# A hybrid decoder step on one core: the first program reordered, and the first norm's scale and shift moved out of it into the attention

## The chip, the cores and the metric

One core of a Trainium2 chip runs the whole kernel. The time is device microseconds of one execution. A core has five engines that run their own instruction lists and meet at semaphores: TensorE (PE; PEld is its weight load), VectorE (DVE), ScalarE (ACT), GpSimd (POOL) and SyncE (SP), which here only issues transfers. All engines read and write the on-chip memory SBUF; TensorE writes its results into eight PSUM banks.

## The reference, cut to what matters

One decoder layer for 1,040 prompt rows (16 learned ones ahead of 1,024) and 64 sample rows, all of width 1024, in float32. What the change touches is the first layer norm, the input projection and the three mixers that read it:

```python
xp = layer_norm(concat([meta, x_prompt]), ln0_g, ln0_b)   # (x - mu) * rsqrt(var + eps) * g + b
z = x @ w_in                       # q, k, v (512 each), 8 forget logits, u (256), p (256)
logf = log_sigmoid(z_f + b_f)
att = softmax(q k^T * scale + cum(logf)_i - cum(logf)_j, causal) @ v
ys  = state-space mixer of u       # y = gelu(scan(u)); y * sigmoid(y @ w_glu + b_glu)
yq  = window means of p (2, 4, 8, 16) minus p, times w_pool
h = layer_norm(alpha * x + concat([att, ys, yq]) @ w_out, ...)
out = layer_norm(alpha * h + moe(h), ...)   # 16 experts, 2 a row
```

Note that the normed rows `x` are used twice: at once by the projection, and much later in the residual `alpha * x`.

## The kernel before, in words

The rows are cut into nine tiles of 128 (`NT = 9`, the last one only 80 rows full). Three programs follow each other, each with its own instruction list for every engine, written out by hand; a program starts when all engines have ended the one before.

**The first program.** For each tile: SP loads the rows into one of six slots `xin`; VectorE takes mean and variance (`stats`), ScalarE the square root, VectorE the reciprocal and the bias (`centre` on DVE), ScalarE writes (x - mu) * rstd in place (`centre` on ACT). TensorE transposes the eight 128-column blocks (`turn_x`), and ScalarE copies the transposed blocks into `xT` and applies gain and shift there, where they are one number per partition (`copy_out`). So the projection reads `xT`. For the residual, GpSimd multiplies the rows in `xin` by the gain and adds the shift, both as 128x1024 operations with vectors spread over all partitions (`gb`), and SP then stores the tile to the DRAM buffer `x_park` and reuses the slot for a later tile.

Between the tiles TensorE runs the projections of u and p (`project(c, u)`, three chunks of 384 columns by four units, the last chunk with 48 columns of padding) and the forget logits (`forget_parts`, `forget_sum`). Then come the value projections (`values(t)`, nine of them), four groups of transposes of the state-space input matrix `Wbd` into `WT` (semaphore `s_wt`, emptied by ScalarE under `s_wc`), 128 small products for the matrix `Tm` (`s_tb`), and sixteen sums of the inputs into states (`s_in`, emptied by ScalarE under `s_ic`), which need GpSimd's rearranged copy `U4` of u (`s_u4`). VectorE makes the matrices (`block_matrices`), a table of rotations (`turns`, ended by `s_tn`), the forget logits (semaphore `s_z`) and their running sums (`s_lf`, `s_cum`), and, when all sixteen sums are in, turns them, scans over time and turns back (ended by `s_xs`). TensorE then makes the eight outputs (`s_y`), ScalarE their GELU (`s_ge`); the pooling mixer's product and the gate follow.

**The second program** is the attention: four pairs of heads, and in each nine row tiles. GpSimd makes, for every tile and head, the diagonal block `diag` (gate sums plus causal mask), four of them deep; VectorE adds scores and gate sums (line 1630, the last piece reads `diag`), ScalarE takes exponentials. Into tiles 2 to 7 of a pair TensorE puts the six projections of the next pair's keys and queries (line 1419), whose weights GpSimd loads at tile 0 (lines 1323, 1324). TensorE's score banks form a ring of four, emptied by VectorE.

**The third program** has the output projection, the residual with the rows of `x_park`, the second norm, the experts and the last norm.

## Time and profile before

| | us |
|---|---|
| median of 3 runs (lowest, highest) | 1066.41 (1066.04, 1068.19) |
| the profiled execution, its own time | 1070.63 |
| its span, first to last instruction | 1068.9 |
| first program ends | 258.1 |
| attention ends | 552 |
| TensorE busy / VectorE / ScalarE / GpSimd | 925.8 / 459.0 / 325.9 / 216.9 |

The profile shows one execution. Times in the rows are from the start of the span. A row of the timeline gives the start, the length, the engine, the line, what is written and read, the shapes and how many instructions it joins; in square brackets stands how long the engine sat idle before it, and what ended that.
### The profile page before, as it was taken

The numbers are of one execution on the slowest core, as the hardware profiler recorded it, in microseconds if no ns is written. First come the engines' busy times: TensorE is split into PE (matmuls) and PEld (weight loads), VectorE is DVE, ScalarE is ACT, GpSimd is POOL, SyncE is SP. The second block draws the span as 40 slices with busy tenths as digits, with TensorE's granted clock in tenths as the row PEclk, the third lists the DMA queues.
The fourth block names the chain that finished last, engine by engine and source line by source line (L and its number), as shares of the span: only waits on it lengthen the run. The fifth ranks groups of instructions, "written<-read, shape, count | busy, mean of one in ns | idle before, by whom it ended". The sixth has DMA issues, their size and how long they took to land. (4 is left out here: it accounts for less than half of the span.)

```text
span 1068.9 us, 13692 instructions
## 1 busy us (share of the span) xinstructions
PE 925.8 (87%) x5012; PEld 587.2 (55%) x5012; DVE 459.0 (43%) x1270; ACT 325.9 (30%) x657; POOL 216.9 (20%) x285
## 2 busy tenths in 40 slices
PE   2689949797989999999889999996799999999491
PEld 2454535364546665666564444442588787878140
DVE  3679956961234434434652243746300100001076
ACT  6462032173123323333532333333112121211322
POOL 4748910000110200200120001232100000000274
PEclk9889969999989999999999999999799999999796
DMA  9513001013992300300731211257776888965382
GB/s 241 152 57 119 1 3 40 29 52 116 423 426 60 96 15 1 101 1 1 241 138 59 80 41 40 97 189 306 257 250 222 308 321 281 373 218 216 127 330 110
DMA packets 63214, 164.05 MB, mean 153 GB/s; under 512 B 19209, under 2 KB 28464, under 8 KB 57640
## 3 DMA queue, kind: packets, MB, share of 16 engines
q1 hardware_dynamic: 57287, 141.90, 38.2%
q0 software_dynamic: 5856, 21.24, 5.5%
q8 instruction: 42, 0.69, 0.3%
q14 instruction: 29, 0.23, 0.1%
HBM read 108.65 MB, written 54.52 MB: 153 GB/s over the span
## 5 line engine op out<-in xcount | busy, mean ns | idle before, releaser
L1419 PE MATMUL banks<-xT,arena 128*128 128x384 f32 (+1 forms) x384 | 126.5, 486 | 10.6 <-DVE mx L1630 4.1
L2086 PE MATMUL banks<-arena,mixT 128*128 128x512 f32 x288 | 131.6, 603 | 0.0
L1419 PEld LDWEIGHTS banks<-xT,arena 128*128 128x128 f32 x384 | 72.8, 193 | 62.3 <-issue 11.5
L2086 PEld LDWEIGHTS banks<-arena,mixT 128*128 128x128 f32 x288 | 52.9, 192 | 56.2 <-issue 56.2
L1538 ACT ACTIVATE arena<-arena,mx 128x128 f32<-128x128 f32 (+8 forms) x72 | 58.5, 813 | 65.6 <-DVE mx L1630 65.0
L2250 PEld LDWEIGHTS banks<-mixT,v_tok 128*128 128x128 f32 x512 | 72.4, 194 | 4.5 <-issue 4.5
L2250 PEld LDWEIGHTS banks<-mixT,arena 128*128 128x128 f32 x512 | 70.4, 190 | 6.8 <-issue 6.8
L2250 PE MATMUL banks<-mixT,v_tok 128*128 128x160 f32 x512 | 73.0, 304 | 0.8 <-ACT mixT L2454 0.8
L2250 PE MATMUL banks<-mixT,arena 128*128 128x160 f32 x512 | 71.7, 300 | 0.8 <-ACT mixT L2454 0.8
L2596 POOL DMA_INDIRECT arena<-y_park,slot_i x18 | 17.2, 956 | 257.7 <-DMA y_park<-arena 252.6
L499 PE MATMUL banks<-xT,v_tok 128*128 128x384 f32 x192 | 66.3, 502 | 2.6 <-ACT xT L691 2.6
L1317 POOL TENSOR_TENSOR diag<-arena,causal 128x128 f32<-128x128 f32 (+1 forms) x72 | 30.3, 430 | 186.9 <-DVE mx L1630 180.4
L2859 DVE TENSOR_TENSOR mixT<-arena,banks 128x320 f32<-128x320 f32 x16 | 7.8, 488 | 131.8 <-PE banks L2250 131.8
L529 PE MATMUL banks<-mixT,xT 128*128 128x512 f32 x144 | 62.6, 593 | 0.0
L2263 PE MATMUL banks<-arena,mixT 128*128 128x512 f32 x128 | 57.6, 593 | 0.9 <-DVE arena L2847 0.9
L1450 PE MATMUL banks<-ident,arena 128*128 128x128 f32 (+1 forms) x360 | 47.6, 265 | 7.9 <-ACT arena L1538 2.9
L499 PEld LDWEIGHTS banks<-xT,v_tok 128*128 128x128 f32 x192 | 36.8, 196 | 30.2 <-issue 5.2
L2847 DVE COPY arena<-banks 128x512 f32<-128x512 f32 x20 | 13.8, 691 | 91.1 <-PE banks L2263 65.5
L1450 PEld LDWEIGHTS banks<-ident,arena 128*128 128x128 f32 (+1 forms) x360 | 36.4, 139 | 24.9 <-issue 9.9
L1439 PE MATMUL banks<-arena 64*128 64x512 f32 (+5 forms) x240 | 48.3, 504 | 1.6 <-DVE mx L1630 1.6
L2562 POOL TENSOR_TENSOR xT<-xT,gb 128x1024 f32<-128x1024 f32 x9 | 21.2, 2354 | 133.7 <-DVE xT L2639 133.7
L1630 DVE CUSTOM_DVE_ANT_0 arena<-banks,arena 128x512 f32<-128x512 f32 (+4 forms) x64 | 36.1, 587 | 27.7 <-PE banks L1439 27.4
(393 smaller groups left out, 1403.3 us busy)
## 6 DMA issues: line engine op xcount, KB each, us to landing
arena<-in_w_down SPq DMA_DIRECT2D x16, 1024.0 KB, 8.1
x_slots<-xT SPq DMA_DIRECT2D x4, 2048.0 KB, 22.4
y_park<-xT SPq DMA_DIRECT2D x4, 2048.0 KB, 42.8
v_tok<-in_w_gate SPq DMA_DIRECT2D x8, 1024.0 KB, 6.0
v_tok<-in_w_up SPq DMA_DIRECT2D x8, 1024.0 KB, 6.2
arena<-in_w_gate SPq DMA_DIRECT2D x8, 1024.0 KB, 5.8
arena<-in_w_up SPq DMA_DIRECT2D x8, 1024.0 KB, 6.9
arena<-x_slots SPq DMA_DIRECT2D x16, 512.0 KB, 5.0
```

What stands on the lines that cost most here:

```text
L499: last = T.matmul(bank[2 + n % 2][:, 0:cn], w[:, k, m * P:(m + 1) * P], xT[:, k, c0:c0 + cn], start=(k == 0), stop=(k == KD - 1))
L529: last = T.matmul(bank[t % 2][:, :], xT[:, k, t * P:(t + 1) * P], w_v[:, k, :], start=(k == 0), stop=(k == KD - 1))
L1317: G.tensor_tensor(diag[:, n % 4, 0:w], nb[i % 2][:, h, t * P:t * P + w], causal[:, 0:w], ALU.add).then_inc(s_dg, 1)
L1419: last = T.matmul(b[:, 0:cn], w[:, k, :], xT[:, k, c0:c0 + cn], start=(k == 0), stop=(k == KD - 1))
L1439: T.matmul(b[0:nq(t), 0:w], qT[i % 2][r, t * P:t * P + nq(t)], kT[i % 2][r, c0:c0 + w], start=True, stop=True).then_inc(s_ring, 1)
L1450: last = T.transpose(b[0:w, j * q:(j + 1) * q], sc[(NT * i + t) % 2][h][0:q, kb * P:kb * P + w], ident[0:q, 0:q])
L1538: S.activation(row, row, ACT.Exp, bias=mx[0:q, 2 * t + h, len(parts(t)) - 1:len(parts(t))], scale=-1.0, accum_out=lsum[0:q, 2 * t + h:2 * ...
L1630: ins = V.tensor_tensor_reduce(sc[(NT * i + t) % 2][h][0:q, k0:k0 + kn], b[0:q, k0 - c0:k0 - c0 + kn], row, -1.0, 3.0e38 if first else mx[ ...
L2086: last = T.matmul(bank[half], mixT[:, k, t * P:(t + 1) * P], w_oh[half][:, k, :], start=(k == 0), stop=(k == KD - 1))
L2250: last = T.matmul(bank[2 * (e % 2) + which][:, CAP * j:CAP * (j + 1)], w_gu[e % 2][:, DW * which + k * DE + j * P:DW * which + k * DE + (j ...
L2263: last = T.matmul(bank[6 + half], hid[e % 6][:, j, 0:MAIN], w_dn[e % 5][:, j * D + 512 * half:j * D + 512 * half + 512], start=(j == 0), s ...
L2562: G.tensor_tensor(h_all[:, t, :], h_all[:, t, :], gb[:, 1, :], ALU.add).then_inc(s_h, 1)
```

## The change

Five things are changed.

1. The first program no longer applies gain and shift to the rows in `xin`: its eighteen GpSimd operations and the two loads of the spread vectors go. SP stores a tile to `x_park` when it is centred, without them.
2. In the attention, GpSimd loads each parked tile back into a piece of the arena, multiplies, adds, and stores it again: one tile behind the diagonals of each of nine row tiles, from tile 2 of the first pair to tile 1 of the second. Two slots are used in turn. The piece is the place of half of the output weights `w_oh[0]`, whose load moves from the start of the attention to the third pair.
3. On VectorE the tile statistics are taken ahead of the state-space parameters (`angles`, `powers`, `input_gain`, `input_matrix`), and the copies of `pick_rows` go to ScalarE. The forget logits move from behind the table of rotations into it, and the running gate sums behind the scan. The reciprocals of `fix` move behind that.
4. On TensorE the transposes of `Wbd` and the products for `Tm` stand ahead of the first two value projections, and three later value projections move one place back: the one after the `Tm` products behind the sixteen sums, `values(7)` behind the fourth output and `values(8)` behind the sixth. ScalarE's copies follow.
5. The last projection chunk has 336 columns and not 384 (the padding is left out).

The core of the diff:

```diff
@@ SP, first program @@
-                sp.dma_start(gb[:, 0, :], bcast_rows(A["ln0_g"], P)).then_inc(s_gain, 16)
-                sp.dma_start(gb[:, 1, :], bcast_rows(A["ln0_b"], P)).then_inc(s_shift, 16)
...
                 for t in range(NT):
-                    sp.wait_ge(s_normed, t + 1)
+                    sp.wait_ge(s_cen, t + 1)
                     sp.dma_start(x_park[t], xin[t % XSL]).then_inc(s_stored[t % XSL], 16)
@@ GpSimd, first program @@
-                for t in range(NT):
-                    pool.wait_ge(s_turned, 2 * t + 2)
-                    G.tensor_tensor(xin[t % XSL], xin[t % XSL], gb[:, 0, :], ALU.mult).then_inc(s_gained, 1)
-                    pool.wait_ge(s_gained, t + 1)
-                    G.tensor_tensor(xin[t % XSL], xin[t % XSL], gb[:, 1, :], ALU.add).then_inc(s_normed, 1)
-
-                pool.wait_ge(s_normed, NT)
+                pool.wait_ge(s_turned, 2 * 6)
@@ TensorE: project, and behind the projections @@
-                    c0, cn = CHUNKS[c]
+                    c0, cn = CHUNKS_T[c]
...
-                pe.wait_ge(s_wv, 16)
-                values(0)
-                values(1)
                 pe.wait_ge(s_bm, 2)
-                pe.wait_ge(s_free, len(ORDER))
                 for b in range(4):
+                    pe.wait_ge(s_free, len(ORDER) - 1 + b if b < 2 else len(ORDER))
...
                     last.then_inc(s_wt, 1)
...
+                    if b == 1:
+                        pe.wait_ge(s_fpc, 3)
+                        blocks_T(0)
+                blocks_T(1).then_inc(s_tb, 1)
+                pe.wait_ge(s_wv, 16)
+                values(0)
+                values(1)
                 pe.wait_ge(s_u4, 1)
...
-                for t in range(3, 8):
+                for t in range(2, 7):
                     values(t)
...
                     if q == 3:
+                        values(7)
+                    if q == 5:
                         values(8)
@@ ScalarE, behind the projections @@
+                for b in range(4):
+                    act.wait_ge(s_wt, b + 1)
+                    S.copy(WT[:, 2 * b:2 * b + 2, :, :].rearrange("p q r n -> p (q r n)"),
+                           bank[2 + b % 2][:, :]).then_inc(s_wc, 1)
                 act.wait_ge(s_z, 1)
...
                 values(0)
                 values(1)
-                for b in range(4):
-                    act.wait_ge(s_wt, b + 1)
...
@@ VectorE: in turns(), and the new functions @@
                     while n < CHP:
+                        if n == P:
+                            logits()
...
+                def logits():
...
+                    dve.wait_ge(s_fs, 3)
+                    for c in range(3):
+                        last = V.tensor_scalar(lf[:, 384 * c:384 * (c + 1)], bank[6][32 * c:32 * c + H, 0:384],
+                                               bfc[:, 0:1], None, ALU.add)
+                    last.then_inc(s_z, 1)
@@ GpSimd, attention @@
+                def load_parked(m):
+                    if m >= 2:
+                        pool.wait_ge(s_po[m % 2], 16 * (m // 2))
+                    pool.dma_start(park[:, 2 + m % 2, :], x_park[m]).then_inc(s_pi[m % 2], 16)
+
+                def normed(m):
+                    if 1 <= m < NT - 1:
+                        load_parked(m + 1)
...
+                    pool.wait_ge(s_pi[m % 2], 16 * (m // 2 + 1))
+                    x = park[:, 2 + m % 2, :]
+                    G.tensor_tensor(x, x, park[:, 0, :], ALU.mult).then_inc(s_pg, 1)
+                    pool.wait_ge(s_pg, m + 1)
+                    G.tensor_tensor(x, x, park[:, 1, :], ALU.add).then_inc(s_ps, 1)
+                    pool.wait_ge(s_ps, m + 1)
+                    pool.dma_start(x_park[m], x).then_inc(s_po[m % 2], 16)
+
+                load_parked(0)
+                load_parked(1)
...
                             n += 1
+                        if 2 <= NT * i + t < NT + 2:
+                            normed(NT * i + t - 2)
                         if t == 0 and i < 3:
                             pool.wait_ge(s_ring, of_rows[i, 5] + 1)
```

How the instructions stand on the engines, at three places. First TensorE, from the last projections (written to banks 2 and 3) to the state sums (to banks 2, 3, 6, 7). Before:

```order
L499 MATMUL banks_3<-xT,v_tok 128x384 x24
L529 MATMUL banks_1<-mixT,xT 128x512 x16
L591 MATMUL banks_3<-ident,arena 128x128 x16
L598 MATMUL banks_5<-arena 32x128 x2
...
L529 MATMUL banks_1<-mixT,xT 128x512 x8
L612 MATMUL banks_3<-arena 128x276 x2
```

and now:

```order
L485 MATMUL banks_3<-xT,v_tok 128x336 x16
L584 MATMUL banks_3<-ident,arena 128x128 x8
L523 MATMUL banks_5<-arena 32x128 x2
...
L584 MATMUL banks_3<-ident,arena 128x128 x8
...
L515 MATMUL banks_1<-mixT,xT 128x512 x16
L602 MATMUL banks_3<-arena 128x276 x2
```

The value projections (128x512) that stood on both sides of the transposes (128x128) and of the `Tm` products (32 rows) now stand behind both, and there are two ahead of the sums and not three.

Second VectorE in the first norm, around tiles 3 to 5 (statistics into `ln_st`, parameters in `par`). Before:

```order
L824 TENSOR_SCALAR ln_st<-ln_st 128x1
L987 COPY pick<-ident 8x8 x4
L828 TENSOR_TENSOR par<-par 128x8
L846 TENSOR_SCALAR par<-par 128x8
...
L855 TENSOR_SCALAR par<-par 128x16
L815 BN_STATS ln_st<-arena 128x6
```

and now:

```order
L822 TENSOR_SCALAR ln_st<-ln_st 128x1
L813 BN_STATS ln_st<-arena 128x6
...
L826 TENSOR_TENSOR par<-par 128x8
L844 TENSOR_SCALAR par<-par 128x8
...
L853 TENSOR_SCALAR par<-par 128x16
L821 RECIPROCAL ln_st<-ln_st 128x1
```

The four copies and the ten operations on the angles stood between tile 3 and the statistics of tile 4; the copies are gone from this engine, and the angles stand behind the statistics of tile 5.

Third GpSimd in the attention's first pair (`diag` are the diagonals, `arena<-in_w_in` the weights of the next pair). Before:

```order
L1317 TENSOR_TENSOR diag<-arena,causal 128x128 x2
L1323 DMA arena<-in_w_in 128x8x128
L1324 DMA arena<-in_w_in 128x8x128
L1317 TENSOR_TENSOR diag<-arena,causal 128x128 x14
```

and now:

```order
L1341 TENSOR_TENSOR diag<-arena,causal 128x128 x4
L1325 TENSOR_TENSOR arena<-arena 128x1024
L1327 TENSOR_TENSOR arena<-arena 128x1024
L1329 DMA x_park<-arena 128x1024
L1341 TENSOR_TENSOR diag<-arena,causal 128x128 x2
L1315 DMA arena<-x_park 128x1024
L1325 TENSOR_TENSOR arena<-arena 128x1024
```

Where fourteen diagonals followed each other, each tile's two are now followed by a load, two operations of 1,024 columns and a store.

## Rows read from the trace of the kernel before

**Rows 1.** Busy time by stretch: length; busy PE, PEld, DVE, ACT, POOL; clock; DMA

```profile
25.90:119.30 93.40, 79.89 (x296) 45.62 (x297) 76.06 (x193) 37.44 (x81) 67.80 (x83) 0.93 0.31 96
...
134.10:149.40 15.30, 0.06 (x1) 0.00 (x0) 8.35 (x26) 7.66 (x9) 4.06 (x9) 0.60 0.00 0
...
171.30:212.80 41.50, 35.20 (x91) 15.57 (x90) 40.74 (x48) 4.21 (x6) 0.00 (x0) 0.95 0.13 45
...
242.00:258.10 16.10, 12.07 (x32) 6.59 (x32) 3.16 (x6) 7.87 (x14) 0.00 (x0) 0.89 0.03 8
```

**Rows 2.** Timeline of TensorE (start, length, what), one projection and one tile's transposes

```profile
75.19 1.04 PE L484 MATMUL banks<-ident,mixT 128*128 128x128 f32 x8
...
90.92 5.43 PE L499 MATMUL banks<-xT,v_tok 128*128 128x384 f32 x16
```

**Rows 3.** Groups of TensorE, first program, by form: the forget-gate products

```profile
L511 PE MATMUL banks<-xT,w_f 128*32 128x384 f32 x48 | 4.9, 532 | 0.0
...
L522 PE MATMUL banks<-arena,pick 128*8 128x384 f32 x6 | 2.4, 488 | 0.3 <-ACT arena L715 0.3
```

**Rows 4.** Timeline of the first norm, around its tile 4

```profile
36.21 2.35 POOL L455 TENSOR_TENSOR mixT<-mixT,gb 128x1024 f32<-128x1024 f32 x1
...
36.38 2.20 DVE L849 TENSOR_SCALAR par<-par 128x8 f32<-128x8 f32 x1
...
43.51 0.20 ACT L681 ACTIVATE ln_st<-ln_st 128x1 f32<-128x1 f32 x1 [8.77 <-DVE ln_st L818]
```

**Rows 5.** Timeline of TensorE between the projections and the state sums

```profile
119.38 13.90 PE L529 MATMUL banks<-mixT,xT 128*128 128x512 f32 x32
...
149.41 1.97 PE L591 MATMUL banks<-ident,arena 128*128 128x128 f32 x8 [15.25 <-ACT arena L768]
...
151.31 5.04 PE L598 MATMUL banks<-arena 128*32 128x128 f32 x128
...
163.25 7.60 PE L612 MATMUL banks<-arena 128*128 128x276 f32 x32
```

**Rows 6.** Timeline of VectorE and ScalarE around the forget logits

```profile
139.76 1.85 DVE L1024 TENSOR_SCALAR gb<-banks,bfc 8x384 f32<-8x384 f32 x3 [0.26 <-DVE en L840]
...
141.65 1.16 ACT L761 ACTIVATE ncum<-gb 8x1152 f32<-8x1152 f32 x1 [21.56 <-DVE gb L1024]
...
156.49 4.00 DVE L1041 COPY arena<-banks 32x512 f32<-32x512 f32 x8 [4.03 <-PE banks L598]
...
160.52 2.19 DVE L1047 SCALAR_TENSOR_TENSOR arena<-ident,dcol,arena 128x128 f32<-128x128 f32 x8
```

**Rows 7.** Groups of GpSimd, first program: the copies into U4

```profile
L468 POOL COPY arena<-arena 32x96 f32<-32x96 f32 (+1 forms) x96 | 46.5, 485 | 4.0
```

**Rows 8.** Timeline of ScalarE, the last four GELUs

```profile
229.67 0.59 ACT L719 COPY v_tok<-banks 128x512 f32<-128x512 f32 x1 [2.38 <-PE banks L529]
...
231.36 10.64 ACT L781 ACTIVATE arena<-banks 32x276 f32<-32x276 f32 x16 [1.11 <-PE banks L633]
```

**Rows 9.** Timeline of the attention, its first two pairs

```profile
290.48 2.50 POOL L1317 TENSOR_TENSOR diag<-arena,causal 128x128 f32<-128x128 f32 x6
...
298.70 8.18 PE L1419 MATMUL banks<-xT,arena 128*128 128x384 f32 x16 [3.39 <-DMA arena<-in_w_in]
...
357.69 0.89 POOL L1323 DMA_DIRECT2D arena<-in_w_in  x1 [13.88 <-PE banks L1419]
...
370.88 0.35 DVE L1630 CUSTOM_DVE_ANT_0 arena<-banks,diag,mx 128x128 f32<-128x128 f32 x1
...
372.85 5.43 PE L1419 MATMUL banks<-xT,arena 128*128 128x384 f32 x16
```

**Rows 10.** DMA issues: operation, number, size, median us from issue to landing

```profile
x_park<-mixT SPq DMA_DIRECT2D x7, 512.0 KB, 2.9
...
arena<-in_w_in POOLq DMA_DIRECT2D x2, 512.0 KB, 12.5
...
x_slots<-xT,slot_i POOLq DMA_INDIRECT x18, 4.8
```

More of the change, by code:

```diff
@@ L531, in values, with blocks_T @@
                     last.then_inc(s_vm, 1)
+                def blocks_T(h):
+                    for q in range(4 * h, 4 * h + 4):
+                        for j in range(L):
+                            for r in range(2):
+                                last = T.matmul(
+                                    bank[4 + h][32 * j:32 * j + 32, (q % 4) * P + 32 * j:(q % 4 + 1) * P],
+                                    Wbd[:, r, q, 32 * (L - 1):32 * L], CA[:, r, q, 0:32 * (L - j)],
+                                    start=(r == 0), stop=(r == 1))
+                    return last
                 pe.wait_ge(s_ids, 1)
@@ L635, in _ @@
                     if q == 3:
+                        values(7)
+                    if q == 5:
                         values(8)
+                pe.wait_ge(s_lf, 1)
+                for t in range(NT):
+                    last = T.transpose(bank[2][:, t * H:(t + 1) * H], lf[:, t * P:(t + 1) * P], ident[0:H, 0:H])
+                last.then_inc(s_lft, 1)
                 pe.wait_ge(s_vc, NT)
@@ L719, in values @@
                     S.copy(v_tok[:, t, :], bank[t % 2][:, :]).then_inc(s_vc, 1)
+                act.wait_ge(s_ids, 1)
+                act.wait_ge(s_wz, 3)
+                for g in range(4):
+                    last = S.copy(pick8[32 * g:32 * g + H, :], ident[32 * g:32 * g + H, 32 * g:32 * g + H])
+                last.then_inc(s_pk, 1)
                 centre(0)
@@ L1000, in _ @@
                 centre(3)
-                pick_rows()
-                angles()
                 stats(4)
@@ L1131, in _ @@
                 dve.wait_ge(s_free, len(ORDER))
+                dve.wait_ge(s_g, 1)
+                chain(V.reciprocal(fix[:, :, :], fix[:, :, :]))
+                for g, w in enumerate((2, 4, 8, 16)):
+                    f = fix[64 * (g % 2):64 * (g % 2) + 64, g // 2, :]
+                    last = V.tensor_scalar(f, f, float(w), None, ALU.mult)
+                chain(last)
                 shifted(la, line[:, 0, :], 1)
```

97 lines of the change are left out of this document (38 added, 59 removed).

## The prediction

> **What bounds the kernel now.** The chain that ended last reaches back only into the third program, so the first program and the attention are read by stretches first: how long a stretch is, and which engine fills it [rows 1]. From the first projection to the last one (25.90 to 119.30) no engine is full: TensorE 79.9 of 93.4 us, VectorE 76.1, GpSimd 67.8. There the timeline shows who waits for whom. GpSimd's gain or shift of one tile lasts 2.35 us, and a VectorE operation on 128x8 numbers that starts in it lasts 2.20 us and ends with it; ScalarE then stands 8.77 us for VectorE's statistics [rows 4]. So VectorE is held up by GpSimd, ScalarE by VectorE, and TensorE, which needs ScalarE's centred rows and copies, by all three.
>
> The second stretch is idle TensorE: 15.3 us between the two first value projections and the transposes of `Wbd`, released by ScalarE's copies out of the banks [rows 1, 5]. The timeline of the other engines says why those are late: ScalarE sits 21.56 us in front of the exponential of the forget logits, for which VectorE's logits end at 141.6; the copies stand behind that in ScalarE's list [rows 6]. In the third (171.30 to 212.80) VectorE is the bound, 40.7 of 41.5 us, while TensorE makes value projections. The fourth ends the program in 16.1 us [rows 1]. In the attention's first pairs TensorE bounds; GpSimd has 2.50 us of diagonals for three tiles and is otherwise idle [rows 9].
>
> **The change, stage by stage.** I compare where each stage ends, since work that only moves inside one costs nothing.
>
> *A, the projections (end 119.3).* With GpSimd's eighteen operations gone, and the angles behind the statistics, I take it that rows, statistics and copies keep ahead of TensorE from the second chunk on, so that the stage lasts as long as TensorE's work. Eight projections at 5.43 us are 43.4; four with 336 columns are 4 x 5.43 x 336/384 = 19.0; six tiles' transposes at 1.04 us are 6.2 [rows 2]; the forget products are 4.9 and 2.4 [rows 3]. Sum 75.9, and 2.5 us for copies that TensorE must still wait for at the tile where ScalarE does its two extra rounds (an estimate, somewhat over one 2.35 us step of the old chain [rows 4]). End 25.9 + 78.4 = 104.3, which is 15.0 earlier. The bounds: TensorE busy 79.9 less 2.7 of padding against 93.4 gives at most 16.2; if the waits on ScalarE and VectorE stay, only the padding and the 2.35 us that VectorE stands in front of an angle operation go, about 5.
>
> *B, to the end of the sixteen sums (170.9).* Before: 119.3 to 170.9, 51.6 us. After, TensorE does sixteen transposes at 1.04 per eight (the 1.97 in the row stands behind the idle time, in a stretch where the granted clock was 0.60 [rows 1, 5]), 2.1; the `Tm` products 5.04; two value projections 13.9; the sums 7.6. Together 28.6, end 132.9. That is 38.0 earlier, of which 15.0 come from A and 23.0 are new: the idle 15.25, a value projection of 13.90/2 = 6.95 that now stands behind, and about 0.9 of transposes. The covers: `U4` costs GpSimd 46.5 us [rows 7]; even if it begins only when eight of the twelve projections are done, two thirds through A near 78, it ends at 125, and the sums want it at 132.9 - 7.6 = 125. VectorE's logits begin at 139.8 [rows 6]; 15.0 earlier, and earlier by the waits for GpSimd too (2 at least, one like that in [rows 4]), makes 122; behind them stand 1.85 of logits and the 4.00 + 2.19 of `Tm` (together 8.0) [rows 6], end 130 to 132. This cover is thin (1 to 3 us): what VectorE lacks there is paid one for one.
>
> *C, VectorE's scan.* 41.5 us before and after [rows 1]: its end moves from 212.8 to 174.8. TensorE has five value projections beside it as before, which fill 35.2 of the 41.5.
>
> *D, outputs and GELU.* Before, the last GELU ended at 242.0, 29.2 after the scan [rows 8]. After, two value projections stand among the outputs. Behind the first of them the fifth GELU starts as before 231.4 - 212.8 = 18.6 after the scan, when its output is there; the sixth output follows in about 1.8 (an estimate: some four products like the sums', which took 7.60/16 each [rows 5]), then value projection 8 with 6.95, the seventh output with 1.8, and two GELUs of 10.64/4 = 2.66: 34.5. So D loses 5.2, rounded. The running sums and `fix` now stand on VectorE here, a few small operations beside 34 us in which VectorE has little else: nothing. *E*, the 16.1 us behind, is unchanged.
>
> First program: 38.0 (A, B and C) less 5.2 is 32.8 earlier; it ends near 225.
>
> *F, the attention.* GpSimd now handles one parked tile behind each tile's diagonals. There are two slots, and a slot's next load waits for its store to have landed, so its loop is serial: the store's landing, 0.9 us to issue the next load (the row of a GpSimd issue [rows 9]) and two operations of 2.35 [rows 4]. The trace has no store of 512 KB from GpSimd. The bounds of the landing: SP's 512 KB store 2.9 us, GpSimd's scatter 4.8, GpSimd's 512 KB weight loads, two together, 12.5 [rows 10]. I take 4.0, since a store alone in the queue is nearest to the first two, which makes 4.0 + 0.9 + 4.7 = 9.6 a tile. In the trace of before GpSimd begins a run of diagonals at 290.5, 2.50 for six [rows 9]; four of them (1.7) and the two operations bring the first parked tile to 296.9. With a first landing of 6 (the first stores meet other transfers) the eighth parked tile is ready at 296.9 + 11.6 + 6 x 9.6 = 366. At that place stand the next pair's first diagonals, the two weight loads (0.89 each), and the ninth tile; with its two operations and 2.7 for issues and diagonals of two tiles, the diagonals of tile 2 in the second pair come out near 376. VectorE reads them at 370.88 and the projection behind it starts at 372.85 [rows 9]: TensorE waits some 4 us. So F loses 4, from 0 at 2.9 to 12 at 4.8 and a first landing of 10. Each earlier tile's diagonals come out within half a microsecond of their need; tile 3's delay lies in front of the weights' wait, which ends at 298.70 in any case [rows 9]. VectorE's attention operations have a PSUM input, and the row of line 1630 is 0.35 us [rows 9] while GpSimd is at work on diagonals; I take no blocking there. Bound from above: all eighteen operations blocking it would be 42 us. The output weights' later load has a pair of time ahead of its use: nothing. The spread gain and shift are also loads that SP no longer issues in the first program; in the attention they come ahead of tile 0.
>
> The Trainium skill, "DMA: Bandwidth & Descriptors", in "Anatomy of one DMA — SWDGE (gpsimd) path", gives a GpSimd transfer about 2.0 us plus its bytes over 436 KB per microsecond, an estimate of 3.2 us for these 512 KB. By that, F would cost nothing and the sum would be four microseconds lower. The trace agrees for the order of the 2.9 us store, and not for the 12.5 us of two loads in flight.
>
> **The sum.** -32.8 + 4 = -28.8. Against the profiled execution, 1070.6, that gives 1041.8; that execution stands 4.2 above the median of the three runs, so the forecast of the median is 1066.4 - 28.8 = **1037.6**.
>
> **The rivals.** *GpSimd keeps up.* Its landings take about 2.9 us [rows 10], the loop 8.5 a tile, and F costs nothing: 1033.6. For it: SP's row is the one with the same bytes and buffer. Against: GpSimd's queue showed no transfer under 4.8.
>
> *The first program gains less.* Projections don't run back to back: each tile's copies (two rounds on ScalarE) and takes of projections share one engine, and A gives about 5 and not 15; 1047.6. For it: ScalarE is the releaser in [rows 4]; and the idle clock (0.60 in the idle stretch) makes a late TensorE slower yet [rows 1, 5]. Against: ScalarE is busy 37.4 of 93.4 us [rows 1].
>
> *GpSimd becomes the bound of the first pair.* If a store takes as long as the scatter or longer while the loads of weights and attention tiles share its queue, each of nine tiles pays. At a landing of 6 us the loop is 11.6, and the ninth tile comes 2.0 x 7 = 14 us later than in my sum: F costs 18, and the time is 1051.6. The kernel is not faster from the point at which F costs 32.8: 28.8 more over seven loops are 4.1 a loop, so a landing over 8.1 us. The weights' row of 12.5 lies beyond it: 8.5 x 7 = 60 more, some 1098. For it: that row [rows 10]. Against: it is two loads together, issued behind each other.
>
> *The change doesn't do what it says*, that is, B's idle time moves and stays: the transposes wait for VectorE's matrices instead. Those are ready before the logits at 139.8 [rows 6] and don't hang on them; I leave this inside the second rival.
>
> **How the numbers follow.** Forecast 1037.6: 50%, with a range of its own of 1032 to 1046 (F from 0 to 12 is 1033.6 to 1045.6; A's bound of 16.2 takes off 1.2 more). GpSimd keeps up, 1033.6: 25%. First program gains less, 1047.6: 13%. GpSimd the bound, 1051.6 and more: 12%, of which a third is slower than before. The range 1029 to 1050 leaves out most of the last and little below. A measurement of this kernel tells about 0.2%, 2 us, from no change: faster 95%, same 1%, slower 4%.
>
> **What would show each step.** In the profile after: the last projection ends near 104 (A); TensorE's idle stretch in front of the transposes is gone and the sums end near 133 (B), with VectorE's last `Tm` operation ahead of it; the scan ends near 175 (C); the last GELU ends 34 behind it (D); the attention starts near 225. In the attention, GpSimd's gain operations stand 9.6 us apart, and VectorE waits for `diag` once, some 5 us, at tile 2 of the second pair (F). Wrong would make it: TensorE waiting for copies between projections; `U4` or `Tm` later than the value projections; waits on `diag` at every tile of the first pair.

## The result, and the profile after

| | before | changed |
|---|---|---|
| median of 4 runs (lowest, highest), us | 1066.22 (1065.71, 1068.19) | 1053.15 (1050.64, 1054.87) |
| the profiled execution (span) | 1070.63 (1068.9) | 1054.87 (1053.1) |
| first program ends | 258.1 | 220.9 |
| attention ends (third program's first product) | 552.4 | 534.0 |

The ratio is 0.9866, 95% interval 0.9843 to 0.9888: 14 us less, where 28.8 were forecast; the time lies 3 us above the range. Executions in the chip's slower state are left out of every median and ratio here and below. The two halves went apart: the first program gained 37.2 us, more than the forecast 32.8; the attention, from 294.3 to 313.1 us, lost 18.8 and not 4. The rest, 2.6 us, is in the third program, which the change doesn't touch; there the last product ended 494.9 us after the first before, 497.2 now, and 496.7 to 500.7 in the twelve experiments; what sets that is not settled.

**The first program.** Busy time by stretch of the changed kernel (columns as in [rows 1]): the projections, then up to the end of the sums, VectorE's scan, and the outputs.

```profile
25.95:103.65 77.70, 74.94 (x296) 43.97 (x297) 56.50 (x200) 37.21 (x81) 40.51 (x96) 1.00 0.36 110
103.65:131.03 27.38, 27.22 (x210) 17.23 (x208) 21.26 (x54) 15.54 (x28) 0.00 (x0) 1.00 0.01 1
131.03:173.05 42.02, 34.96 (x83) 15.39 (x81) 40.73 (x48) 4.72 (x8) 0.00 (x0) 0.96 0.00 1
173.05:204.00 30.95, 30.95 (x126) 21.23 (x127) 21.90 (x41) 20.16 (x31) 0.00 (x0) 0.94 0.18 62
```

TensorE fills the first two stretches, 74.9 of 77.7 and 27.2 of 27.4 us, where it had 79.9 of 93.4 and then, behind two value projections, 15.3 us of nothing. TensorE's timeline:

```profile
89.35 14.47 PE L485 MATMUL banks<-xT,v_tok 128*128 128x384 f32 x48
...
104.41 0.66 PE L584 MATMUL banks<-ident,arena 128*128 128x128 f32 x4 [0.16 <-ACT arena L698]
...
123.59 7.60 PE L602 MATMUL banks<-arena 128*128 128x276 f32 x32
...
173.05 1.24 PE L618 MATMUL banks<-arena 128*128 128x260 f32 x2 [7.06 <-DVE arena L1072]
...
220.93 1.32 PE L1450 MATMUL banks<-xT,arena 128*128 128x384 f32 x2 [2.66 <-PEq L114]
```

The projections end at 103.8 (119.3 before), the wait of 15.25 us [rows 5] is 0.16, the sums end at 131.2 (170.9), and the outputs begin at 173.05 (212.8). The last row's wait is the change of programs. VectorE and ScalarE:

```profile
107.58 1.85 DVE L956 TENSOR_SCALAR gb<-banks,bfc 8x384 f32<-8x384 f32 x3
...
123.83 2.19 DVE L1042 SCALAR_TENSOR_TENSOR arena<-ident,dcol,arena 128x128 f32<-128x128 f32 x8
```

```profile
200.91 5.31 ACT L777 ACTIVATE arena<-banks 32x276 f32<-32x276 f32 x8 [1.11 <-PE banks L619]
```

The logits begin at 107.6, where 139.8 stood before and 122 was forecast; the last operation for `Tm` ends at 126, five microseconds ahead of the sums' end. So the cover that I called thin was not. VectorE is busy 56.5 us in the stretch of the projections, where it was 76.1 in [rows 1]. The operation of [rows 4] that ended with GpSimd's and took 2.20 us is line 847 now, in the groups of VectorE (count, busy, mean ns, idle before):

```profile
L847 DVE TENSOR_SCALAR par<-par 128x8 f32<-128x8 f32 x1 | 0.2, 171 | 0.0
```

0.17 us. The last GELU ends at 206.2, 33.2 after the scan.

**The attention.** GpSimd's timeline from the first parked tile on (L1325 is the gain, L1327 the shift, L1329 the store, L1315 the next load, L1341 the diagonals):

```profile
256.33 2.35 POOL L1325 TENSOR_TENSOR arena<-arena 128x1024 f32<-128x1024 f32 x1
...
261.41 0.60 POOL L1329 DMA_DIRECT2D x_park<-arena  x1 [0.30 <-POOL arena L1327]
...
274.63 0.56 POOL L1315 DMA_DIRECT2D arena<-x_park  x1 [11.73 <-DMA x_park<-arena]
...
280.29 0.59 POOL L1329 DMA_DIRECT2D x_park<-arena  x1 [0.30 <-POOL arena L1327]
280.89 0.89 POOL L1341 TENSOR_TENSOR diag<-arena,causal 128x128 f32<-128x128 f32 x2
292.27 0.55 POOL L1315 DMA_DIRECT2D arena<-x_park  x1 [10.49 <-DMA x_park<-arena]
...
298.50 0.88 POOL L1341 TENSOR_TENSOR diag<-arena,causal 128x128 f32<-128x128 f32 x2
301.28 0.55 POOL L1315 DMA_DIRECT2D arena<-x_park  x1 [1.91 <-DMA x_park<-arena]
```

GpSimd stands at line 1315, in front of the load of the next tile, until the store that frees the slot, that of the tile two places before, has landed: 11.73 us, then 10.49, and from the third store on 1.8 to 3.6. Everything behind that line in GpSimd's list stands too: the operations on a tile that is long there, and the diagonals, which begin at 280.9 and 298.5. VectorE waits for these, in the view of waits (engine, operation, for whom: sum, times, longest):

```profile
DVE arena L1661 <- POOL diag L1341: 24.8, 4, 13.8
```

Three of the four stand in the first pair (2.3, 5.4 and 13.8 us, ended at 262.6, 281.5 and 299.1); the fourth, 3.3 us, is at tile 2 of the second pair, where step F had its only one. TensorE waits behind VectorE (timeline, and stretches with columns as above, the last two numbers the share of the DMA engines and GB/s):

```profile
265.13 7.33 PE L1450 MATMUL banks<-xT,arena 128*128 128x384 f32 x16 [5.36 <-DMA arena<-in_w_in]
...
301.98 1.98 PE L1510 MATMUL banks<-ident,rl 128*64 128x128 f32 x16 [10.79 <-ACT arena L1555]
```

```profile
252.40:265.10 12.70, 5.66 (x36) 2.89 (x34) 6.88 (x33) 7.68 (x21) 9.65 (x11) 0.89 1.01 424
265.10:289.30 24.20, 23.25 (x100) 14.19 (x101) 5.79 (x18) 2.68 (x6) 6.74 (x6) 0.92 1.00 419
289.30:302.00 12.70, 1.91 (x26) 1.50 (x24) 2.20 (x10) 2.41 (x5) 7.40 (x8) 0.78 0.47 105
```

What the two slow stores have in common is read in the last columns: up to 289 the sixteen DMA engines are full, at 420 GB/s. It is SP's twelve transfers that fill `x_slots` and `y_park` (20 MB), issued at the start of the attention, before the change too; the last of them has landed at 291.8. The issue of one of SP's small loads behind them lasts 37.63 us:

```profile
251.11 37.63 SPq L1378 DMA_DIRECT2D gcol<-in_ln_g  x1
```

It ends at 288.7, and the stores after it take 2.9 to 6.2 us. All nine stores of the changed kernel took, from issue to landing:

```profile
DMA to landing us min/median/max: 2.9/3.6/12.9
```

The first took 12.9 and the second 11.7. How much of the 12.9 is due to the two weight loads in GpSimd's own queue, which landed at 265.1 and 271.2 only, is not known; ahead of the second stood one load.

### The profile page after: what moved, and what is told of

It reads as the page before. It is cut to its first block and busy times, and to the rows that moved or that the text cites. A ratio compares the mean times of both kernels' runs of the same rounds, so it can differ in the third digit from the quotient of the medians.

```text
span 1053.1 us, 13715 instructions
## 1 busy us (share of the span) xinstructions
PE 921.8 (88%) x5012; PEld 583.7 (55%) x5012; DVE 433.3 (41%) x1266; ACT 327.6 (31%) x662; POOL 220.7 (21%) x303
## 5 line engine op out<-in xcount | busy, mean ns | idle before, releaser
L485 PE MATMUL banks<-xT,v_tok 128*128 128x384 f32 (+1 forms) x192 | 63.7, 488 | 2.6 <-ACT xT L683 2.6
L1341 POOL TENSOR_TENSOR diag<-arena,causal 128x128 f32<-128x128 f32 (+1 forms) x72 | 29.9, 431 | 128.4 <-DVE mx L1661 123.4
L2878 DVE COPY arena<-banks 128x512 f32<-128x512 f32 x20 | 13.8, 692 | 91.1 <-PE banks L2294 65.5
L454 POOL COPY arena<-arena 32x96 f32<-32x96 f32 (+1 forms) x96 | 40.5, 422 | 51.4 <-PE banks L470 47.4
```

The costliest lines, as they stand in the source:

```text
L454: last = G.tensor_copy(U4[32 * j:32 * j + 32, 4 * m + q, c0:c1], uT[32 * q:32 * q + 32, m, L * c0:L * c1].rearrange("p (c j) -> p c j", j= ...
L485: last = T.matmul(bank[2 + n % 2][:, 0:cn], w[:, k, m * P:(m + 1) * P], xT[:, k, c0:c0 + cn], start=(k == 0), stop=(k == KD - 1))
L1341: G.tensor_tensor(diag[:, n % 4, 0:w], nb[i % 2][:, h, t * P:t * P + w], causal[:, 0:w], ALU.add).then_inc(s_dg, 1)
```

## The experiments

Each was timed beside the kernel before on the same chip, whose median was then 1068.2 to 1068.9; so a difference between two kernels is that of their ratios, times 1066, and not of their medians. A pair is counted from TensorE's one 128x80 transpose at its start to that of the next pair, in the one trace that each kernel has.

| kernel | median us | ratio to before (95%) | first pair, second pair, us |
|---|---|---|---|
| before | 1066.2 | 1 | 77.5, 71.4 |
| changed | 1053.2 | 0.9866 (0.9843 to 0.9888) | 92.8, 73.2 |
| e1_pair1 | 1038.6 | 0.9709 (0.9684 to 0.9735) | 78.2, 71.4 |
| e2_fills_late | 1038.6 | 0.9716 (0.9696 to 0.9736) | 72.4, 74.3 |
| e3_ops_only | 1039.9 | 0.9717 (0.9689 to 0.9746) | 78.2, 71.4 |
| e4_dma_only | 1047.4 | 0.9794 (0.9772 to 0.9816) | 88.6, 71.4 |
| e5_order_back | 1045.4 | 0.9779 (0.9756 to 0.9802) | 78.2, 71.4 |
| e6_logits_late | 1040.3 | 0.9732 (0.9712 to 0.9753) | 78.6, 71.4 |
| e7_pair1_values7 | 1029.0 | 0.9632 (0.9616 to 0.9648) | 77.6, 71.4 |
| e8_gpsimd_back | 1050.8 | 0.9834 (0.9816 to 0.9853) | 79.0, 71.4 |
| e9_order_logits_back | 1055.2 | 0.9874 (0.9851 to 0.9897) | 77.1, 71.4 |
| e10_ops_first | 1065.6 | 0.9964 (0.9943 to 0.9985) | 86.7, 87.4 |
| e11_fills_late_values7 | 1030.4 | 0.9638 (0.9613 to 0.9664) | 72.7, 76.2 |
| e12_fills_third_values7 | 1029.8 | 0.9641 (0.9618 to 0.9665) | 72.9, 74.3 |

### What the attention lost

Two theories: the stores land late under SP's fills (S), or GpSimd's loop costs wherever it stands (G).

**The parked tiles in the second pair.**

```diff
-                        if 2 <= NT * i + t < NT + 2:
-                            normed(NT * i + t - 2)
+                        if NT + 2 <= NT * i + t < 2 * NT + 2:
+                            normed(NT * i + t - NT - 2)
```

> The parked tiles are handled one pair of heads later (tile 2 of the second pair to tile 1 of the third), where SP's filling of x_slots and y_park has ended. In the changed kernel the attention took 313.1 us from its first projection to its end, 18.8 more than before: 1.7 in the first projections, 15.3 in the first pair, 1.7 in the second. Theory S (the first stores land late, 11 to 13 us, because SP's fills hold the DMA engines): the first pair goes back to about 77.5 us, the stores land in 3 to 4 us, the loop is near 9 us a tile, which the second pair (71.4 us for nine tiles, 7.9 each) hides up to its end and then pays some 2 to 6 us: about 1040 us, 1037 to 1044. Rival G (the loop on GpSimd, two operations of 2.35 us and a round trip a tile, is what costs, in whichever pair): the loss of 15 to 19 us moves to the second pair, the time stays at 1051 to 1056.

Measured 1038.6, 16.7 us below the changed kernel. The two pairs, as stretches:

```profile
253.50:331.60 78.10, 68.42 (x435) 43.10 (x435) 31.47 (x117) 25.68 (x59) 15.72 (x28) 0.96 0.53 197
331.60:403.00 71.40, 67.25 (x471) 43.09 (x471) 31.07 (x114) 23.87 (x55) 52.39 (x49) 1.00 0.41 140
```

The first pair is back at 78.2, and the second, with nearly the whole loop in it (GpSimd busy 52.4 of 71.4 us), takes what it took before to a tenth. GpSimd's loop of 9 us a tile is longer than TensorE's 7.9, but its last store is issued only 3.7 us into the third pair; one diagonal came 0.8 us late there, and the third pair takes 71.4 us as before. The stores landed in 2.9 to 5.0 us (the last, behind two weight loads, in 8.9). S is right, and my expectation that the second pair would pay 2 to 6 us was too high.

**SP's fills behind the first pair**, the parked tiles where the change put them.

```diff
-                for n, (dst, r0, span) in enumerate(((x_slots, 0, E * CAP // 2), ...
...
                     if i >= 1 and i < 3:
                         rows(i + 1)
+                    if i == 1:
+                        for n, (dst, r0, span) in enumerate(((x_slots, 0, E * CAP // 2), ...
```

> SP's six plus six fills of x_slots and y_park from xT (some 20 MB) are issued behind the first pair and not at its start; the parked tiles stay in the first pair. Theory S: the stores of the first parked tiles land in about 3.5 us, the waits of 11.7 and 10.5 us on GpSimd shrink to about 2, the first pair returns to some 75 to 78 us and the wait of 5.4 us for the next pair's weights shrinks as well; the fills then stand beside the second pair, where only two weight loads are wanted: 1032 to 1042 us. Rival G (the loop itself costs): the waits on GpSimd for stores shrink little and the time stays at 1050 to 1056. Rival W (the fills' bandwidth has to be paid somewhere): the loss moves to the second pair, 1048 to 1056.

Measured 1038.6. GpSimd's waits for stores fall from 33.5 us to 14.2, none over 3.2:

```profile
POOL arena L1315 <- DMA x_park<-arena: 14.2, 7, 3.2
```

```profile
251.80:324.30 72.50, 66.37 (x436) 42.07 (x436) 31.54 (x117) 25.56 (x59) 55.01 (x52) 1.00 0.36 125
324.30:398.60 74.30, 67.29 (x472) 43.06 (x472) 30.95 (x114) 23.89 (x55) 17.77 (x29) 1.00 0.87 348
```

The first pair takes 72.4 us, five less than before the change: TensorE's wait for the next pair's weights, 3.39 us in [rows 9], is gone too, and its clock is 1.00. GpSimd's last store now comes 7.5 us into the second pair, and there VectorE waits once for a diagonal:

```profile
DVE arena L1662 <- POOL diag L1341: 4.5, 1, 4.5
```

That is the late diagonal of step F, forecast at "some 5 us". It is not the fills' price, which now begin beside it: e12, whose fills stand in the third pair, has the same wait of 4.5 us and the same 74.3 for the second pair, and its third pair, with the fills, takes 71.4. So the third theory, that the fills' bandwidth has to be paid elsewhere, isn't borne out; the second pair's 2.9 us are the loop's tail. In e2's first pair VectorE waits three times more, 9.0 us together, where the prediction had half a microsecond; that pair takes 1.0 more than the pairs that have neither parked tiles nor fills (71.4).

**Half of the loop at a time.** e3 leaves out all stores, and the loads after the first two tiles; e4 leaves out both operations; in both, the residual's rows stay without gain and shift.

```diff
 e3                                        e4
-  load_parked(m + 1)                     -  G.tensor_tensor(x, x, park[:, 0, :], ALU.mult)
...
-  pool.dma_start(x_park[m], x)           -  G.tensor_tensor(x, x, park[:, 1, :], ALU.add)
```

> GpSimd does its two operations behind each tile's diagonals as in the changed kernel, on the two first parked tiles over and over, but neither loads nor stores anything further (the residual's rows stay without gain and shift). Theory S: GpSimd is never held up, the first pair goes back to 77 to 79 us: 1034 to 1040 us. Rival G, in the form that the 42 us of operations cost VectorE or the diagonals: the first pair stays above 85 us, 1045 us or more.

> GpSimd loads and stores each parked tile as in the changed kernel, with the same waits, but does neither of the two operations (the residual's rows stay without gain and shift). Theory S: the first two stores still take 11 to 13 us and hold up the diagonals behind them; the load of the next tile no longer has two operations of 4.7 us to run under, so the first pair loses about 10 to 15 us: 1045 to 1053 us. Rival G: without the operations little is lost, 1034 to 1038 us.

Measured 1039.9 and 1047.4: the operations by themselves cost nothing (first pair 78.2, as in e1 without them), so GpSimd's operations don't hold up VectorE here. In e1's second pair VectorE's 128x128 operations that read `diag` last 0.351 us on average beside one of them and 0.349 without. The transfers by themselves cost 10 us of the first pair. GpSimd's timeline of e4:

```profile
255.89 0.58 POOL L1325 DMA_DIRECT2D x_park<-arena  x1
...
275.18 0.56 POOL L1315 DMA_DIRECT2D arena<-x_park  x1 [17.80 <-DMA x_park<-arena]
275.73 0.55 POOL L1325 DMA_DIRECT2D x_park<-arena  x1
...
292.33 0.55 POOL L1315 DMA_DIRECT2D arena<-x_park  x1 [15.16 <-DMA x_park<-arena]
```

The first store is issued at 255.9 and waited for until 275.2, the second from 275.7 until 292.3: they took 19.0 and 16.3 us to land, not the 12.9 and 11.7 of the changed kernel, where they were issued 5.5 and 4.6 us later behind the operations and were waited for until 274.6 and 292.3. So the stores are late without the 42 us of operations too, and here the earlier issue brought no earlier landing.

**The wait moved behind the operations.** If the wait for a store stands in the way of work that is ready, the load can be issued behind the two operations:

```diff
-                    if 1 <= m < NT - 1:
-                        load_parked(m + 1)
...
                     pool.dma_start(x_park[m], x).then_inc(s_po[m % 2], 16)
+                    if 1 <= m < NT - 1:
+                        load_parked(m + 1)
```

> The changed kernel with one line moved: GpSimd issues the load of the next parked tile, and waits for the store before it to land, behind the two operations on the tile that is already there and not ahead of them. Theory S with the queue's order (GpSimd stands at the store's landing with the next tile's work and diagonals behind it): the second store is issued near 268 and not 280 us, the diagonals that came at 280.9 come near 275 and those at 298.5 near 292; the first pair loses some 9 us and not 15: 1045 to 1049. Rival (the landings add up whatever stands between them): 1051 to 1055.

Measured 1065.6, 10.4 us above the changed kernel: both expectations missed. GpSimd's timeline shows why:

```profile
274.03 0.55 POOL L1315 DMA_DIRECT2D arena<-x_park  x1 [5.99 <-DMA x_park<-arena]
274.59 0.88 POOL L1341 TENSOR_TENSOR diag<-arena,causal 128x128 f32<-128x128 f32 x2
286.20 2.35 POOL L1323 TENSOR_TENSOR arena<-arena 128x1024 f32<-128x1024 f32 x1 [10.73 <-DMA arena<-x_park]
...
296.84 2.34 POOL L1323 TENSOR_TENSOR arena<-arena 128x1024 f32<-128x1024 f32 x1 [3.57 <-DMA arena<-x_park]
```

The store's wait has shrunk as expected (5.99), the diagonals come at 274.6, and the first pair loses 6.1 us less, 86.7. But now nothing lies between the issue of a load and its use: GpSimd waits for the load, 10.73 us under the fills and 3.57 in the first round behind them. The loop grows from 9.0 to some 10.6 us a tile; its last round takes 14.2, with 5.34 us of waiting for a load that has the two weight loads beside it. The last store stands 18.6 us into the second pair, where the changed kernel's stands 6.3 us; there VectorE waits for two diagonals:

```profile
347.86 0.35 DVE L1661 CUSTOM_DVE_ANT_0 arena<-banks,diag,mx 128x128 f32<-128x128 f32 x1 [5.31 <-POOL diag L1341]
...
359.74 0.35 DVE L1661 CUSTOM_DVE_ANT_0 arena<-banks,diag,mx 128x128 f32<-128x128 f32 x1 [10.38 <-POOL diag L1341]
```

and that pair takes 87.4 us, 16 more than before. So one thing of G holds: the loop's own length counts where its end reaches into the next pair. What 1.6 us a tile would cost by themselves, in a pair without fills, was not timed. I had left the covered side of the wait out of the expectation.

### What the first program gained

**The old order on TensorE and ScalarE**, on the kernel e1: two value projections first, the transposes and `Tm` behind them, a third value projection, the sums; ScalarE's copies behind the exponentials.

```diff
+                values(0)
+                values(1)
                 for b in range(4):      # transposes of Wbd
...
                 blocks_T(1).then_inc(s_tb, 1)
-                values(0)
-                values(1)
+                values(2)
```

> On the kernel with the parked tiles in the second pair: TensorE and ScalarE have their old order again behind the projections (two value projections, the transposes of Wbd, the Tm products, a third value projection, then the sums; ScalarE's copies of the transposes behind the exponentials of the forget logits). The forget logits keep their new early place on VectorE (107.6 us in the changed kernel). Theory L (the 15.25 us in which TensorE stood idle came from late logits, so the early logits alone remove it): no idle time, only the third value projection's 6.95 us move ahead of the sums and the scan; the time rises by about 7 us over the 1038.6 of that kernel, 1043 to 1048. Rival O (the order of the copies behind the exponentials removed it): the idle time of 10 to 15 us returns beside the 7, 1054 to 1062.

Measured 1045.4, by the ratios 7.5 us above e1, as theory L had it. TensorE's timeline:

```profile
118.46 1.15 PE L587 MATMUL banks<-ident,arena 128*128 128x128 f32 x8 [0.29 <-ACT arena L765]
```

The wait for the copies is 0.29; what is paid is the third value projection's 7 us.

**The logits late**, with the new order:

```diff
-                        if n == P:
-                            logits()
...
                 turns()
+                logits()
```

> On the same kernel: the forget logits stand behind the table of rotations again, as before the change; everything else is new. Their end moves from 109.4 to about 121.5 us, ScalarE's three passes over them to 122 to 128, and its copies of the sums behind these. Theory L in its strict form (the early logits carry all of the gain): the sums end 10 us or more later, 1048 us or more. Rival O (the new order on TensorE and ScalarE has taken the logits off the way): only the wait for ScalarE is left, the sums end 3 to 6 us later, 1041 to 1045.

Measured 1040.3, by the ratios 2.5 us above e1, with intervals that overlap, and a little under rival O's range. TensorE's only wait over 0.2 us from the projections to the sums is inside the sums, which end at 131.8 (131.2 in the changed kernel):

```profile
125.90 5.85 PE L602 MATMUL banks<-arena 128*128 128x276 f32 x24 [2.02 <-ACT mixT L770]
```

Neither edit alone brings the idle time back.

**Both:**

> On the kernel with the parked tiles in the second pair: both edits of the two runs before at once, the old order on TensorE and ScalarE and the forget logits behind the table of rotations. Each alone cost 7.5 and 2.3 us. Theory T (either of the two is enough to remove the idle time of 15.25 us, since it stood in the old order behind late logits): now it returns, the logits end near 121.5 us and ScalarE's passes at 128, so that TensorE waits 8 to 12 us ahead of the transposes' second half; 1054 to 1062 us. Rival (the idle time came from GpSimd's operations, which are gone): the two costs add up, 1047 to 1050.

Measured 1055.2, 17.6 above e1, where the two costs would add up to 10: theory T. TensorE waits again where it did before:

```profile
127.03 1.97 PE L587 MATMUL banks<-ident,arena 128*128 128x128 f32 x8 [8.85 <-ACT arena L765]
```

8.85 us in front of the transposes' second half, and the granted clock is 0.50 behind it (1.97 us for eight transposes). It is 8.85 and not 15.25 [rows 5], since with the rest of the change in place VectorE reaches the late logits 22.4 us sooner (117.4 against 139.8) and TensorE the end of the projections only 15.9. So the change removes this idle time twice over: with the rest of it in place, the early logits, or the new order with the copies ahead of the exponentials, would have done alone.

**GpSimd's operations back in the first program**, nothing parked in the attention: parts 1 and 2 of the change, backwards. The core:

```diff
+                for t in range(NT):
+                    pool.wait_ge(s_turned, 2 * t + 2)
+                    G.tensor_tensor(xin[t % XSL], xin[t % XSL], gb[:, 0, :], ALU.mult).then_inc(s_gained, 1)
+                    pool.wait_ge(s_gained, t + 1)
+                    G.tensor_tensor(xin[t % XSL], xin[t % XSL], gb[:, 1, :], ALU.add).then_inc(s_normed, 1)
...
-                        if 2 <= NT * i + t < NT + 2:
-                            normed(NT * i + t - 2)
```

> The changed kernel with GpSimd's eighteen operations on the gain and shift back in the first program (with the loads of the spread vectors and the stores that wait for them), and no parked tiles in the attention; the new orders stay. Theory P (GpSimd's operations hold up VectorE, and that TensorE): the last projection ends at 112 to 120 us and not at 103.7, VectorE's rotations and Tm later than the value projections, the first program ends 12 to 25 us later than in the changed kernel; with a free attention 1045 to 1060. Rival R (the new order of the statistics and the narrow last chunk alone gave stage A its 15 us): the last projection stays at 103 to 107 us, and the time is 1034 to 1040.

Measured 1050.8: P is right. TensorE's timeline:

```profile
99.60 14.47 PE L499 MATMUL banks<-xT,v_tok 128*128 128x384 f32 x48
...
135.77 7.71 PE L616 MATMUL banks<-arena 128*128 128x276 f32 x32 [1.77 <-POOL arena L468]
```

The projections end at 114.1 and not 103.8, and the sums wait 1.77 us for `U4`; the first program ends at 233.8, 12.9 later. That VectorE is what GpSimd holds up shows in the operation of [rows 4], which lasted 0.17 us in the changed kernel (line 861 here) and lasts as long as GpSimd's again:

```profile
41.55 2.35 POOL L455 TENSOR_TENSOR arena<-arena,gb 128x1024 f32<-128x1024 f32 x1
...
41.65 2.27 DVE L861 TENSOR_SCALAR par<-par 128x8 f32<-128x8 f32 x1
```

VectorE's logits begin at 123.4, where they begin at 107.6 in the changed kernel. So 10.3 of stage A's 15.5 us are GpSimd's operations; the other 5.2 are left for the order and the narrow chunk, of which neither was undone alone. Of the whole 37.2 us, GpSimd's operations are 12.9. Beside the changed kernel (0.9834 against 0.9866, intervals that overlap) this says that the move of gain and shift, as the change placed it, gave nothing that can be measured: it gained 12.9 us in the first program and lost 15.6 in the attention (297.5 us in e8, 313.1 in the changed kernel). One pair later (e1) the same move is worth 13 us.

**A value projection in the scan's shadow.** TensorE waits 7.06 us for the scan, and two value projections stand in its way later.

```diff
-                for t in range(2, 7):
+                for t in range(2, 8):
                     values(t)
...
                     if q == 3:
-                        values(7)
-                    if q == 5:
                         values(8)
```

> On the same kernel: one value projection (7) is back ahead of the outputs, in the 7.06 us in which TensorE waits for VectorE's scan; only the eighth stands among the outputs. If the two value projections among the outputs cost what my sum gave them (33.2 us from the scan to the last GELU against 29.2 before), the time falls by 3 to 5 us, to 1034 to 1036. Rival: ScalarE's GELUs set the end of that stage in any case, less than 1.5 us, 1037 to 1039.

Measured 1029.0, 8.2 us below e1, more than expected. The wait is gone and the last GELU ends at 199.1, not 206:

```profile
172.76 0.71 PE L618 MATMUL banks<-arena 128*128 128x260 f32 x2 [0.20 <-DVE arena L1068]
```

```profile
188.32 10.76 ACT L775 ACTIVATE arena<-banks 32x276 f32<-32x276 f32 x16 [1.11 <-PE banks L619]
```

The first program ends 5.6 us earlier. Another 0.6 are in the first pair. The remaining 1.7, in the first projections of the attention (29.9 us as before the change, not 31.6), can't be put down to this edit, since e4 has them without it (see the last section).

**Both together.** e11 is e2 with this edit; in e12 the loop of fills stands at `if i == 2`, behind the load of `w_oh[0]`.

> The parked tiles in the first pair, SP's fills behind it, and value projection 7 ahead of the outputs: both gains of the runs before. If they add up (8 us off the kernel with late fills), 1027 to 1033; if the clock or the weights take one back, 1034 to 1038.

> The same with the fills one pair later again, behind the load of the output weights in the third pair. With the fills behind the first pair, the second pair took 74.3 us and not 71.4. If that is the price of the fills beside the projections' weights, the third pair pays it here (74 us) and the time is the same, 1026 to 1033; if the parked tiles' tail and the fills together cost it, both pairs take 71.4 to 72.5 and the time falls to 1023 to 1029; if the fills' end is late for the third program, which waits for them, it rises above 1035.

Measured 1030.4 and 1029.8: inside the ranges, and the same as e7 within the intervals. Freeing the first pair of the fills is worth 5 us there. The parked tiles' tail costs 2.9 of them in the second pair (74.3 in e12). In e11 that pair takes 76.2, and the other 1.9 are the clock, which was 0.98 over the pair and 1.00 in e12:

```profile
317.10:393.40 76.30, 69.05 (x472) 43.98 (x472) 31.05 (x114) 23.90 (x55) 18.03 (x29) 0.98 0.85 339
317.20:391.40 74.20, 67.26 (x471) 43.04 (x471) 30.91 (x114) 23.88 (x55) 17.67 (x29) 1.00 0.20 66
```

The reason given for e12's range was not the right one: the fills cost the third pair nothing (71.4). Some 1029 us, 3.6% below the kernel before and 2.4% below the changed one, is the best that was found, and three versions reach it.

## Why the prediction was off, step by step

In the profiled executions the gain is 15.8 us, where 28.8 were forecast: the first program gained 4.4 more than its 32.8, the attention lost 14.8 more than its 4, and the third program, left out of the sum, lost 2.6.

*A* was right: the projections end at 103.8, forecast 104.3. *B*: the sums end at 131.2, forecast 132.9; the `Tm` products took 3.9 us at the full clock, not the 5.04 of the row behind the idle time. Its reading was right in the cause (the late logits in front of the copies) and incomplete: e5 and e6 show that either half of the cure is enough. *C*: 41.9 us from the end of the sums to the scan's, as before between the same events; right. *D* lost 4.0, forecast 5.2. *E* was 1.4 us shorter, which was not followed up. I hadn't asked whether D's loss was needed at all; the 6 us of TensorE's slack in C, which my own text states, were the answer (e7).

*F* is the step that failed, and in it one term, the landing of a store: "I take 4.0, since a store alone in the queue is nearest to the first two", and "a first landing of 6 (the first stores meet other transfers)". From one gain operation to the next, the timeline shows 18.9, 17.6, then 9.0, 8.9, 8.9. The loop and its serial wait were right, also its length when undisturbed (9.0; 9.6 forecast), and e2 and e12 show the late diagonal of 4.5 us at tile 2 of the second pair. The two landings under the fills took 12.9 and 11.7, 7 to 8 us longer each than I took, together 15. The two pairs lost 15.3 and 1.8 us, 13 more than the 4; the last 1.7 of the 18.8 are in the first projections, which F did not touch. The place was wrong with the size: I had the delay at the second pair's start alone, and three diagonals of the first pair were late. Moving the fills (e2) or the loop (e1) away from each other takes away the two long landings and 16 to 17 us of the time.

The size was in the rows. I took the 12.5 us of the two weight loads [rows 10] for "two loads together, issued behind each other". The same line over the whole trace of before reads:

```profile
DMA to landing us min/median/max: 4.9/5.3/10.2
```

The median is 5.3, with the same two loads together in every pair; only the first pair's, under SP's fills, are slow. Read by pair, it says that 512 KB which GpSimd moved before the fills' end took 10.2 us and, for the second load, 14.7; and the DMA column of the stretches (as in [rows 1]) over the first pair would have given the reason. Two landings of 12 in place of 6 and 4 make F 18, as the third rival had it, though by seven landings of 6 and not by two of 12; its 12% were too few for the one row of the trace that stood in the right place. Two smaller readings were wrong: the scatter's 4.8 us are a median, and GpSimd's fastest one landed in 3.4, so the argument against a short landing had no ground; and the 0.35 us of line 1630 in [rows 9] stand between two diagonals of GpSimd, not beside one. That there is no blocking in the attention was shown only by e3 and the averages from e1. By its own terms the upper end of F is 12.8 and not 12, which changes nothing.

The Trainium skill, "DMA: Bandwidth & Descriptors", "Anatomy of one DMA — SWDGE (gpsimd) path", gave an estimate of 3.2 us for this store. The fastest store of the changed kernel took 2.9 us and the median one 3.6, so the trace agrees where the fills are not beside it; under the fills the first took 12.9, and there the measurement decides.

## What to carry to other kernels

Before a transfer is moved, look at what the DMA engines do in the stretch where it goes, and take its duration from a transfer in that stretch, not from the fastest or the median of the trace. A wait in an engine's list costs what stands behind it: count it at each place, and look also at what the wait covers before it is moved (e10). When two edits remove one idle time, undo each alone and both together; only then it is seen which of them is needed.

## What was not expected of the hardware

TensorE's granted clock at the start of the attention differs between traces whose first programs are alike. The first four microseconds of the attention in the changed kernel, and in e4 (columns as above, the clock third from last):

```profile
220.90:224.90 4.00, 3.97 (x7) 2.20 (x8) 0.00 (x0) 0.00 (x0) 1.63 (x3) 0.57 0.57 159
```

```profile
222.20:226.20 4.00, 4.00 (x13) 2.41 (x14) 0.00 (x0) 0.00 (x0) 1.60 (x3) 1.00 0.58 163
```

Both come behind a wait of 2.67 us. The 0.57 is a mean of the two levels, 1.2 and 2.4 GHz (0.50 and 1.00). With it the first projections take 31.6 us, at 1.00 they take 29.9, as before the change. They took 31.6 in e1 to e3, e5, e6, e8 and e10, and 29.9 in e4, e7, e9, e11 and e12; what decides it was not found. The first program of e4 is that of the changed kernel, and each kernel has one trace, so the difference may lie in the execution and not in the kernel. It is 1.7 of the 18.8 us that the attention lost.
